# A class of its own for experts with at most 64 rows, in two 64-column groups of TensorE

## The chip, the cores and the metric

The kernel runs on one core of a Trainium2 chip. The metric is the device time of one execution in microseconds; the time before is the median of three runs. The profile is one further execution, taken by the hardware profiler.

## The reference, cut to what matters

A two-layer transformer step over 384 tokens (128 context, 256 latent; width 1024) in fp32. Layer 0 ends in a dense SwiGLU, layer 1 in a top-2-of-8 expert SwiGLU, and the change touches only the latter:

```python
logits = (t @ w_router).astype(jnp.float32)
top_v, top_i = lax.top_k(logits, TOP_K)          # TOP_K = 2, 8 experts
...
for e in range(N_EXPERTS):
    out = out + combine[:, e:e + 1] * swiglu(t, w_gu[e], w_d[e])
def swiglu(x, w_gu, w_d):
    g, u = jnp.split(x @ w_gu, 2, axis=-1)       # 1024 -> 2 x 2816
    return (jax.nn.silu(g) * u) @ w_d            # 2816 -> 1024
```

Only the rows that chose an expert need its product. With the reference's inputs the eight experts get 98, 55, 106, 107, 71, 38, 158 and 135 rows (768 = 2 x 384). Each expert's weights are 34.6 MB, read once.

## The kernel before, in words

**The stream.** All weights come as chunks of 128 x 2048 fp32 (1 MB, two DMAs of 512 KB, issued by SP at L542) through a ring `raw` of RING = 6 buffers. SP issues chunk n once TensorE has finished chunk n-6 (`s_pe`). An expert has 33 chunks: 22 of gate and up (blocks of 512 columns, four chunks a block; the last block of 256 has two chunks with narrower pieces) and 11 of down.

Each product is three matmuls (`three`, L1576 to L1578): hi by hi, hi by lo, lo by hi, of 128 x 128 by 512 columns; a chunk is 12 of them for one tile of 128 rows.

**Experts and classes.** Routing on DVE counts the rows per expert and writes a class number into `ntile`. SHAPES lists the classes: (1, 0) up to 128 rows, (1, 1) up to 160, (2, 0) up to 256, (3, 0) up to 384. In (1, 1) the rows past 128 (at most 32) go another way: `xsum` and `hsum`, unsplit fp32, are multiplied with the `raw` chunk itself in four groups of 32 columns of the array (L2105, L2138), which write four quarters of the PSUM partitions; only chunks 0 and 1, which are split before the class is known, are taken as `whi` and `wlo`. `by_tiles` writes, on each of PE, ACT and DVE, the code of every class one after the other, and within a class that of the eight experts; after an expert, `leave` reads the next expert's class and branches to that class's code for it. The next expert of the same class follows directly.

**Order within an expert.** PE goes through 22 gate/up chunks; after the fifth of each next block it transposes the finished gated block (`turn`, L2072), and ACT and DVE bring it to `hhi` and `hlo`. Then 11 down chunks, between which the next expert's gathered rows are transposed (`gathered`, L2051). ACT and DVE split two chunks of the next expert before they leave one. At the end ACT copies the result to `f` (L933), GpSimd scatters it to `y_rows` (L734) and gathers the rows of the expert after next to `hx` (L709). `s_glo`, `s_ye`, `s_yst`, `s_more` and `s_mored` order the next expert's start.

Of the kernel before, what the change touches and what calls it, by code (L numbers as in the profile page):

```python
# [37 lines left out]
ROWS = 4  # L38
SCALE = HD ** -0.5
QUARTER = P // 4  # L40
SHAPES = [(1, 0), (1, 1), (2, 0), (3, 0)]

# [72 lines left out]
def build(nc, x_prompt, x_sample, cache_k, cache_v, c, c_ctx, w_ada, b_ada, norm_g, w_in, w_out, rpb,  # L115
          g_v, w_s, b_s, w_conv, w_ffn_gu, w_ffn_d, w_router, w_moe_gu, w_moe_d,
          y_prompt, y_sample, new_k, new_v, h_rows, y_rows, rpb_rows):
    with ExitStack() as ctx:
# [323 lines left out]
        def units(b):  # L442

            return min(2 * b + 2, GU_B)
# [30 lines left out]
        def gated_part(T, t, b):  # L475

            return gated[:, 0:block_width(b)] if T == 1 else f[:, t, 0:block_width(b)]

        def rest_width(b):
# [270 lines left out]
        def _(act):  # L750
# [125 lines left out]
            def gathered(e, i):  # L876

                act.wait_ge(s_ga, KT * e + 4 * i + 4)
                act.activation(xhi[:, 4 * i:4 * i + 4, 0:P], gathered_banks(i), ACT.Copy).then_inc(s_ghi, 4)

            def expert(T, quarter, e):

                n0, k = PLACE["exp", e, 0], e + 1

                def silu(b):
# [178 lines left out]
        def _(dve):  # L1064
# [181 lines left out]
            def near_sum(t):  # L1246
# [4 lines left out]
                dve.scalar_tensor_tensor(out=hx[:, t, :], in0=y_near[1][:, t, :], scalar=near_gates[:, 1, t:t + 1],  # L1251
                                         in1=hx[:, t, :], op0=ALU.mult, op1=ALU.add).then_inc(s_near_d, 1)

            def expert(T, quarter, e):

                n0, k = PLACE["exp", e, 0], e + 1
                over = e if quarter else None

# [248 lines left out]
            for t in range(NT):  # L1507
# [62 lines left out]
        def _(pe):  # L1570
# [474 lines left out]
            def gathered(e, i):  # L2045

                if i == 0:
                    pe.wait_ge(s_hx, 16 * NT * e)
                for k in range(4):
                    kt = 4 * i + k  # L2050
                    ins = pe.transpose(ps[:, 6 + i, P * k:P * k + P], hx[:, 0, P * kt:P * kt + P], ident[:, :])  # L2051
                ins.then_inc(s_ga, 4)

            def expert(T, quarter, e):

                n0, k = PLACE["exp", e, 0], e + 1

                def turn(b):
# [220 lines left out]
```

## Time and profile before

| | |
|---|---|
| median of 3 runs | 1615.28 us (1614.29 to 1617.17) |
| the profiled execution | 1618.33 us, span of its trace 1616.6 us |
| TensorE busy | 1557.5 us, 96% of the span |
| VectorE, ScalarE busy | 1031.7 us (64%), 872.7 us (54%) |
| expert stage | from 759.5 us to the end |
| moved by DMA | 425.02 MB, mean 263 GB/s |

Times of rows are in us from the start of the span. PE is TensorE's matmul side, PEld its weight load, DVE VectorE, ACT ScalarE, SP the engine that issues the chunk loads. One fp32 matmul shows as two records. A matmul's duration includes its run through the array, so the distance of starts tells the rate. "issue" is idle time for which the profile shows no releaser.

### The profile page before, as it was taken

How to read it: one execution, taken by the hardware profiler on the slowest of the kernel's cores; microseconds unless marked ns; L12 is line 12 of the kernel's file. 1: busy time of each engine (PE TensorE's matmuls, PEld its weight loads, DVE VectorE, ACT ScalarE, POOL GpSimd, SP SyncE). 2: the span in 40 equal slices, each digit the busy share in tenths (PEclk: the TensorE clock that was granted, in tenths of full speed). 3: DMA queues.
4: the chain of work that ended last, by engine and by line, in shares of the span. 5: the costliest groups of instructions: out<-in, count | busy, mean ns of one | idle time of the engine just before them, and what ended most of it. 6: DMA issues, size and time to landing. Idle time of an engine off the chain costs nothing.

```text
span 1616.6 us, 24317 instructions
## 1 busy us (share of the span) xinstructions
PE 1557.5 (96%) x10076; PEld 1229.6 (76%) x10076; DVE 1031.7 (64%) x935; ACT 872.7 (54%) x886; POOL 164.9 (10%) x180
## 2 busy tenths in 40 slices
PE   6999999999999999998999999999999999999994
PEld 3677777777777778777888888888888878778872
DVE  1445574333422464557888889888888966666665
ACT  2435453222322454545777777777777755555553
POOL 2400000000000220012102030110303010001001
PEclk9999999999999999999999999999999999999998
DMA  9973325666665473233999999999999987878871
GB/s 330 335 264 143 94 84 170 222 210 211 229 241 201 126 246 112 85 125 129 381 371 382 383 367 387 372 379 376 379 383 372 388 323 254 272 265 302 271 283 69
DMA packets 214762, 425.02 MB, mean 263 GB/s; under 512 B 21986, under 2 KB 62946, under 8 KB 214528
## 3 DMA queue, kind: packets, MB, share of 16 engines
q1 hardware_dynamic: 200448, 397.99, 69.4%
q0 software_dynamic: 13056, 22.71, 4.7%
q10 hardware_dynamic: 1136, 2.64, 0.4%
q8 instruction: 84, 1.38, 0.4%
q14 instruction: 38, 0.31, 0.1%
HBM read 418.56 MB, written 22.41 MB: 273 GB/s over the span
## 4 chain that ended last, share of the span: by engine, by line
PE 90%; DVE 4%; DMA 2%; SPq 2%; ACT 1%; issue 1%; POOL 0%; DVEq 0%; ACTq 0%; POOLq 0%
PE ps L1576 26%; PE ps L1578 25%; PE ps L1577 25%; PE ps L2105 3%; PE ps L1620 2%; DMA raw<-in_w_in_dram 1%; SPq L542 1%; PE ps L2138 1%; PE ps L2072 1%; DVE wlo L1072 1%; PE ps L1736 1%; ACT whi L760 1%; PE ps L1767 1%; PE ps L1751 1%; DVE f L1166 1%
## 5 line engine op out<-in xcount | busy, mean ns | idle before, releaser
L1072 DVE TENSOR_TENSOR wlo<-raw,whi 128x2048 fp32r<-128x2048 f32 x327 | 745.4, 2289 | 319.2 <-ACT whi L760 228.1
L760 ACT ACTIVATE whi<-raw 128x2048 fp32r<-128x2048 f32 x327 | 626.6, 1918 | 448.2 <-PE ps L1578 222.1
L1576 PE MATMUL ps<-whi,xhi 128*128 128x512 f32 (+1 forms) x1352 | 538.1, 398 | 5.0 <-DVE xlo L1150 2.3
L1578 PE MATMUL ps<-whi,xlo 128*128 128x512 f32 (+1 forms) x1352 | 524.2, 388 | 0.0
L1577 PE MATMUL ps<-wlo,xhi 128*128 128x512 f32 (+1 forms) x1352 | 524.0, 388 | 0.0
L1576 PEld LDWEIGHTS ps<-whi,xhi 128*128 128x128 f32 x1352 | 255.2, 189 | 68.8 <-issue 15.1
L1578 PEld LDWEIGHTS ps<-whi,xlo 128*128 128x128 f32 x1352 | 255.1, 189 | 53.2
L1577 PEld LDWEIGHTS ps<-wlo,xhi 128*128 128x128 f32 x1352 | 255.5, 189 | 47.8 <-issue 0.5
L1576 PE MATMUL ps<-whi,hhi 128*128 128x512 f32 x484 | 193.9, 401 | 2.6 <-DVE wlo L1072 2.6
L1578 PE MATMUL ps<-whi,hlo 128*128 128x512 f32 x484 | 189.4, 391 | 0.0
L1577 PE MATMUL ps<-wlo,hhi 128*128 128x512 f32 x484 | 189.4, 391 | 0.0
L1576 PEld LDWEIGHTS ps<-whi,hhi 128*128 128x128 f32 x484 | 91.2, 189 | 24.1 <-issue 3.5
L1578 PEld LDWEIGHTS ps<-whi,hlo 128*128 128x128 f32 x484 | 91.3, 189 | 19.7
L1577 PEld LDWEIGHTS ps<-wlo,hhi 128*128 128x128 f32 x484 | 91.4, 189 | 18.1 <-issue 0.2
L734 POOL DMA_INDIRECT y_rows<-f,lidx x24 | 35.4, 1476 | 655.9 <-ACT f L933 400.4
L1620 PE MATMUL ps<-raw,cS 128*32 128x512 f32 x384 | 52.2, 659 | 15.5 <-DMA raw<-in_w_ada_dram 15.5
L709 POOL DMA_INDIRECT hx<-h_rows,lidx x21 | 44.3, 2111 | 9.4 <-issue 6.1
L1620 PEld LDWEIGHTS ps<-raw,cS 128*32 128x32 f32 x384 | 10.2, 114 | 43.2 <-issue 23.3
L905 ACT ACTIVATE hhi<-ps 128x512 fp32r<-128x512 f32 (+1 forms) x48 | 26.3, 548 | 26.9 <-PE ps L2072 13.6
L992 ACT ACTIVATE pr<-ps 128x512 f32<-128x512 f32 (+1 forms) x36 | 19.8, 557 | 37.6 <-PE ps L1578 37.5
L1110 DVE TENSOR_TENSOR f<-ps,f 128x512 f32<-128x512 f32 x12 | 8.3, 690 | 49.1 <-PE ps L1620 49.1
L2105 PE MATMUL ps<-raw,xsum 128*32 128x128 f32 x1280 | 39.0, 274 | 0.0
(245 smaller groups left out, 1090.2 us busy)
## 6 DMA issues: line engine op xcount, KB each, us to landing
raw<-in_w_moe_gu_dram SPq DMA_DIRECT2D x352, 512.0 KB, 5.6
raw<-in_w_moe_d_dram SPq DMA_DIRECT2D x176, 512.0 KB, 5.1
raw<-in_w_ada_dram SPq DMA_DIRECT2D x96, 512.0 KB, 5.1
raw<-in_w_in_dram SPq DMA_DIRECT2D x44, 512.0 KB, 5.3
raw<-in_w_ffn_gu_dram SPq DMA_DIRECT2D x44, 512.0 KB, 6.8
raw<-in_w_ffn_d_dram SPq DMA_DIRECT2D x22, 512.0 KB, 7.0
raw<-in_w_out_dram SPq DMA_DIRECT2D x16, 512.0 KB, 4.2
bias<-rpb_rows POOLq DMA_DIRECT2D x32, 96.0 KB, 4.9
```

Source lines behind the costliest of these rows:

```text
L542: sp.dma_start(to, of).then_inc(s_raw[n % RING], 16)
L709: pool.indirect_dma_start(out=hx[:, i, :], out_offset=None, in_=h_rows[:, :], in_offset=bass.IndirectOffsetOnAxis(ap=lidx[:, e, i:i + 1], ...
L734: pool.indirect_dma_start(out=y_rows[:, :], out_offset=bass.IndirectOffsetOnAxis(ap=lidx[:, e, i:i + 1], axis=0), in_=f[:, i, :], in_offse ...
L760: act.activation(whi[m % SPL][:, :], raw[n % RING][:, :], ACT.Copy).then_inc(s_hi, 1)
L905: act.activation(hhi[:, kts.start:kts.stop, 0:P * T], ps[:, bank, 0:P * T * len(kts)].rearrange("p (k n) -> p k n", k=len(kts)), ACT.Copy) ...
L992: act.activation(pr[:, t, 512 * b:512 * b + width], ps[:, t, 0:width], ACT.Copy).then_inc(s_pr, 1)
L1072: dve.tensor_tensor(wlo[n % RING][:, :], raw[n % RING][:, :], whi[NTH[n] % SPL][:, :].bitcast(F32), ALU.subtract).then_inc(s_lo, 1)
L1576: pe.matmul(out, a_hi, w_hi, start=start, stop=False)
L1577: pe.matmul(out, a_hi, w_lo, start=False, stop=False)
L1578: return pe.matmul(out, a_lo, w_hi, start=False, stop=stop)
L1620: ins = pe.matmul(ps[32 * k:32 * k + 32, bank, :], cS[:, 4 * h + k, :], w[:, k, :], start=(h == 0), stop=(h == 1))
L2105: ins = pe.matmul(o, xsum[:, kt, P:P + QUARTER], m, start=(kt == 0 and i == 0), stop=(kt == KT - 1 and i == len(weights) - 1))
```

## The change

A fifth class (0, 0), for at most HALF = 64 rows, is put first in SHAPES. Such an expert's chunks from the third on are not split: PE multiplies `raw` with `xsum` and `hsum` in two groups of 64 columns of the array, the two halves of a block's columns side by side in the two halves of the PSUM partitions. ACT keeps silu and the final copies, DVE the products and plain copies. The semaphores that splits would have raised are raised in one step. At its end each engine splits the next expert's two first chunks as before. The routing gets one more comparison. The diff, cut to its core:

```diff
-SHAPES = [(1, 0), (1, 1), (2, 0), (3, 0)]
+HALF = P // 2
+SHAPES = [(0, 0), (1, 0), (1, 1), (2, 0), (3, 0)]
...
@@ scalar
+            def half_expert(e):
+                n0, k = PLACE["exp", e, 0], e + 1
+                act.sem_inc(s_morea, KT)
+                act.sem_inc(s_hhi, FK)
+                for b in range(LAST_BLOCK + 1):
+                    act.wait_ge(s_pe, n0 + gate_done(b) + 1)
+                    act.wait_ge(s_ht, FK * k + 4 * (b - 1) if b > 1 else FK * k)
+                    act.activation(half_gated(b), half_gate(b), ACT.Silu
+                                   ).then_inc(s_sg, units(b) - units(b - 1) if b else 2)
+                act.sem_inc(s_hi, N_FFN - 2)
+                state["n"] = n0 + N_FFN
...
+                upto(n0 + N_FFN + 1)
...
+                act.wait_ge(s_pe, n0 + N_FFN)
+                for j in range(2):
+                    ins = act.activation(f[0:HALF, 0, 512 * j:512 * j + 512],
+                                         ps[HALF * j:HALF * j + HALF, DOWN_BANK, :], ACT.Copy)
+                ins.then_inc(s_ye, 1)
...
@@ vector
+            def half_expert(e):
+                n0, k = PLACE["exp", e, 0], e + 1
+                dve.wait_ge(s_glo, KT * (e + 1))
+                for i in range(2):
+                    ins = dve.tensor_copy(xsum[:, 4 * i:4 * i + 4, 0:HALF], gathered_banks(i)[:, :, 0:HALF])
+                ins.then_inc(s_mored, KT)
...
+                for b in range(LAST_BLOCK + 1):
+                    mult(b)
+                    copy(b)
+                dve.sem_inc(s_lo, N_FFN - 2)
+                state["n"] = n0 + N_FFN
...
+                upto(n0 + N_FFN + 1)
...
-            chain(dve.tensor_scalar(cnt[:, :], ps[:, 3, 0:NE], float(P), None, ALU.is_gt))
+            chain(dve.tensor_scalar(cnt[:, :], ps[:, 3, 0:NE], float(HALF), None, ALU.is_gt))
+            chain(dve.scalar_tensor_tensor(out=cnt[:, :], in0=ps[:, 3, 0:NE], scalar=float(P), in1=cnt[:, :],
+                                           op0=ALU.is_gt, op1=ALU.add))
...
@@ tensor
+            def half_expert(e):
...
+                def weights(c, k):
+                    n = n0 + c
+                    if c < 2:
+                        pe.wait_ge(s_lo, NTH[n] + 1)
+                        return [v.bitcast(F32) for v in halves(n, k)]
+                    pe.wait_ge(s_raw[n % RING], 32 * (n // RING + 1))
+                    return [raw[n % RING][:, :].rearrange("p (k n) -> p k n", k=k)]
+                def gate_up_chunk(c):
+                    b, part = divmod(c, 4)
+                    if c == 0:
+                        pe.wait_ge(s_mored, KT * (e + 1))
...
+                    for kk in range(4):
+                        kt = 4 * (part % 2) + kk
+                        for i, v in enumerate(ws):
+                            for j in range(2):
...
+                                ins = pe.matmul(o, xsum[:, kt, 0:HALF], m, start=(kt == 0 and i == 0),
+                                                stop=(kt == KT - 1 and i == len(ws) - 1))
+                    pe_done(ins)
...
+                        for j in range(2):
+                            ins = pe.matmul(ps[HALF * j:HALF * j + HALF, DOWN_BANK, :], hsum[:, kt, 0:HALF],
+                                            w[:, i, 512 * j:512 * j + 512], start=(kt == 0), stop=(kt == FK - 1))
...
             def expert(T, quarter, e):
+                if T == 0:
+                    return half_expert(e)
```

## Rows read from the trace of the kernel before

**Rows 1.** The page's part 1: busy time, share of the span, instructions of each engine
```profile
PE 1557.5 (96%) x10076; PEld 1229.6 (76%) x10076; DVE 1031.7 (64%) x935; ACT 872.7 (54%) x886; POOL 164.9 (10%) x180
```

**Rows 2.** Windows, experts 1, 5 and 6: length, busy per engine, clock, DMA share, GB/s
```profile
853.30:946.80 93.50, 93.28 (x426) 76.82 (x425) 82.27 (x48) 70.50 (x48) 10.47 (x6) 1.00 1.03 378
...
1227.60:1321.20 93.60, 93.60 (x428) 77.11 (x427) 82.75 (x48) 70.43 (x48) 12.93 (x6) 1.00 1.03 379
1321.70:1459.00 137.30, 134.17 (x1388) 104.72 (x1387) 84.97 (x61) 71.52 (x54) 6.02 (x6) 0.98 0.77 261
```

**Rows 3.** Timelines of PE, ACT and DVE from expert 5 to 6: start, length, operation, idle before
```profile
1318.16 0.39 PE L1576 MATMUL ps<-whi,hhi 128*128 128x512 f32 x1
1318.84 0.39 PE L1576 MATMUL ps<-whi,hhi 128*128 128x512 f32 x1
...
1324.85 1.06 PE L2032 MATMUL ps<-ident,hx 32*128 32x32 f32 x8 [3.13 <-issue]
...
1327.29 0.63 PE L1576 MATMUL ps<-whi,xhi 128*128 128x512 f32 x1
...
1328.57 0.63 PE L1576 MATMUL ps<-whi,xhi 128*128 128x512 f32 x1
...
1321.76 1.02 ACT L933 ACTIVATE f<-ps 128x1024 f32<-128x1024 f32 x1 [0.74 <-PE ps L1578]
1327.53 1.91 ACT L760 ACTIVATE whi<-raw 128x2048 fp32r<-128x2048 f32 x1 [4.75 <-issue]
...
1321.05 2.29 DVE L1072 TENSOR_TENSOR wlo<-raw,whi 128x2048 fp32r<-128x2048 f32 x1 [0.42 <-ACT whi L760]
1326.02 0.42 DVE L1210 COPY xsum<-ps 128x256 f32<-128x256 f32 x1 [2.68 <-PE ps L2032]
```

**Rows 4.** Windows with the DMA full: the head, and three parts of expert 1
```profile
34.00:44.00 10.00, 8.98 (x63) 5.96 (x61) 3.32 (x6) 2.54 (x3) 0.00 (x0) 0.83 1.05 387
875.00:895.00 20.00, 20.00 (x94) 16.56 (x93) 18.46 (x12) 15.15 (x11) 0.00 (x0) 1.00 1.05 387
906.00:912.00 6.00, 6.00 (x28) 4.94 (x28) 5.27 (x5) 4.89 (x5) 0.00 (x0) 1.00 1.02 404
898.00:904.00 6.00, 6.00 (x29) 4.95 (x27) 5.38 (x4) 4.08 (x3) 0.00 (x0) 1.00 1.06 354
```

**Rows 5.** Windows of 1 us from expert 5 to 6: the last three columns are clock, DMA, GB/s
```profile
1324.00:1325.00 1.00, 0.15 (x2) 0.15 (x2) 0.00 (x0) 0.00 (x0) 0.69 (x2) 0.64 1.03 383
...
1327.00:1328.00 1.00, 1.00 (x4) 0.81 (x3) 0.00 (x0) 0.47 (x1) 0.69 (x2) 0.50 0.48 150
...
1331.00:1332.00 1.00, 1.00 (x29) 0.78 (x32) 0.00 (x0) 0.00 (x0) 0.14 (x1) 0.94 0.23 34
...
1336.00:1337.00 1.00, 1.00 (x28) 0.75 (x19) 1.00 (x1) 0.97 (x1) 0.00 (x0) 1.00 0.98 121
```

**Rows 6.** Timeline of PE in expert 6: fp32 matmuls in four groups of 32 columns
```profile
1331.22 0.43 PE L2105 MATMUL ps<-whi,xsum 128*32 128x128 f32 x8
...
1334.74 1.93 PE L2105 MATMUL ps<-raw,xsum 128*32 128x128 f32 x64
```

**Rows 7.** SP's waits, expert 1 and then expert 5 to 6: total, times, longest
```profile
SPq L542 <- PE ps L1578: 64.6, 33, 2.4
...
SPq L542 <- PE ps L2105: 12.3, 1, 12.3
```

**Rows 8.** Timeline of PE in the head: one chunk of w_ada, four groups of 32 columns
```profile
18.97 1.94 PE L1620 MATMUL ps<-raw,cS 128*32 128x512 f32 x8 [1.29 <-DMA raw<-in_w_ada_dram]
...
29.70 1.07 PE L1620 MATMUL ps<-raw,cS 128*32 128x512 f32 x8 [2.37 <-DMA raw<-in_w_ada_dram]
```

**Rows 9.** Timelines of DVE, ACT and PE at the start of expert 0
```profile
750.98 0.17 DVE L1533 SCALAR_TENSOR_TENSOR cnt<-ps,cnt 128x8 f32<-128x8 f32 x1
...
759.38 1.92 ACT L760 ACTIVATE whi<-raw 128x2048 fp32r<-128x2048 f32 x1 [0.74 <-issue]
...
759.50 0.50 PE L1576 MATMUL ps<-whi,xhi 128*128 128x512 f32 x1 [1.54 <-DVE xlo L1203]
```

More of the change, by code:

```diff
@@ L477, in gated_part, with half_gated, half_gate, half_up @@
             return gated[:, 0:block_width(b)] if T == 1 else f[:, t, 0:block_width(b)]
+        DOWN_BANK = 4
+        def half_gated(b):
+            return gated[:, 256 * (b % 2):256 * (b % 2) + block_width(b) // 2]
+        def half_gate(b):
+            return ps[:, 2 * (b % 2), 0:block_width(b) // 2]
+        def half_up(b):
+            w = block_width(b) // 2
+            return ps[:, 2 * (b % 2) + 1, 0:w] if b < LAST_BLOCK else ps[:, 2 * (b % 2), w:2 * w]
         def rest_width(b):
@@ L879, in gathered @@
                 act.activation(xhi[:, 4 * i:4 * i + 4, 0:P], gathered_banks(i), ACT.Copy).then_inc(s_ghi, 4)
+            def half_expert(e):
[9 more added lines that the diff above has]
+                state["n"] = n0 + N_FFN
+                for q in range(FK // 2):
+                    if e < NE - 1 and q in GATHER_AT:
+                        gathered(e + 1, GATHER_AT[q])
+                    if e == NE - 1 and 7 <= q < 7 + NT:
+                        near_sum(q - 7)
+                upto(n0 + N_FFN + 1)
+                if e == 0:
+                    act.wait_ge(s_scat, 16 * 2 * NT)
+                else:
+                    act.wait_ge(s_yst, 16 * NT * e)
+                act.sem_inc(s_ye, NT - 1)
+                act.wait_ge(s_pe, n0 + N_FFN)
[3 more added lines that the diff above has]
+                ins.then_inc(s_ye, 1)
             def expert(T, quarter, e):
+                if T == 0:
+                    return half_expert(e)
                 n0, k = PLACE["exp", e, 0], e + 1
@@ L1252, in near_sum, with mult, copy @@
                                          in1=hx[:, t, :], op0=ALU.mult, op1=ALU.add).then_inc(s_near_d, 1)
+            def half_expert(e):
[4 more added lines that the diff above has]
+                ins.then_inc(s_mored, KT)
+                def mult(b):
+                    dve.wait_ge(s_sg, GU_B * k + units(b))
+                    dve.wait_ge(s_pe, n0 + up_done(b) + 1)
+                    dve.tensor_tensor(half_gated(b), half_gated(b), half_up(b), ALU.mult
+                                      ).then_inc(s_pm, units(b) - units(b - 1) if b else 2)
+                def copy(b):
+                    n = ktiles(b) // 2
+                    dve.wait_ge(s_hhi, FK * (k + 1))
+                    dve.wait_ge(s_ht, FK * k + 4 * b + ktiles(b))
+                    for i in range(n):
+                        ins = dve.tensor_copy(hsum[:, 4 * b:4 * b + 2 * n, 0:HALF].rearrange("p (j i) n -> p i j n", i=n)[:, i],
+                                              ps[:, 6 + b % 2, P * i:P * i + P].rearrange("p (j n) -> p j n", j=2))
+                    ins.then_inc(s_hlo, ktiles(b))
+                for b in range(LAST_BLOCK + 1):
[3 more added lines that the diff above has]
+                state["n"] = n0 + N_FFN
+                for q in range(FK // 2):
+                    if e < NE - 1 and q in GATHER_AT:
+                        gathered(e + 1, GATHER_AT[q])
+                    if e == NE - 1 and 7 <= q < 7 + NT:
+                        near_sum(q - 7)
+                upto(n0 + N_FFN + 1)
             def expert(T, quarter, e):
+                if T == 0:
+                    return half_expert(e)
                 n0, k = PLACE["exp", e, 0], e + 1
@@ L2054, in expert @@
             def expert(T, quarter, e):
+                if T == 0:
+                    return half_expert(e)
                 n0, k = PLACE["exp", e, 0], e + 1
```

43 lines of the change are left out of this document (added).

## The prediction

> **What bounds the kernel now.** First the page's part 1 [rows 1]: TensorE is busy 96% of the span. Then the table by expert [rows 2]: there it is busy all the time at full granted clock, but the DMA's share is 1.03 as well, so busy shares alone can't say what a faster expert is worth. The durations can. The copy of an expert's result (L933) cuts the stage: each of experts 1 to 5 takes 93.6 us (expert 0 about as much), whatever its row count (98, 55, 106, 107, 71, 38), with PE busy all of it: TensorE is the bound. Expert 6 (158 rows; 7 has 135) takes 137 us. The counts are the reference's routing on its own inputs. The 93.6 us are worked out thus: three matmuls of 512 columns start every 0.68 us [rows 3], 0.227 each, and 33 chunks x 12 are 89.9 us; 22 transposes of the hidden block and 8 of the next rows do the rest. The DMA moves 378 GB/s meanwhile and is held back only by TensorE: in expert 1's time SP waits 33 times for a chunk's last matmul, 64.6 us in all [rows 7]. What it can do alone stands in [rows 4]: 387 GB/s both in the head, where nothing holds it, and in the gate/up part of an expert; 404 in the down part, whose rows are longer; 354 at the last, narrow gate/up block. A chunk is 1.049 MB, so 2.71, 2.60 and 2.96 us against TensorE's 2.73 us plus transposes. The cover of TensorE is thin: the DMA is the next bound, 3 to 4 us per expert behind.
>
> **The change part by part.** Only experts 1 and 5 have at most 64 rows: two experts of eight change class. Let t0 be the end of the expert before (PE's last matmul).
>
> *Matmuls.* Removed: 12 x 33 matmuls, per expert, and all but two splits on ACT (1.92) and DVE (2.29). Added: per gate/up chunk 4 steps of two groups at once, 64 columns of the array each, 256 columns streamed in fp32; chunks 0 and 1 have 8 steps (whi and wlo); a down chunk has 2 steps of 512. The nearest row is the over class: four groups of 128 columns; 16 such steps (chunks 0 and 1, whi and wlo) fill 1331.22 to 1334.74, 0.22 us each [rows 6]. By columns 0.43 us a step, 1.72 a chunk, 3.44 for chunks 0 and 1: 60 us per expert instead of 90. Loads then bound it. Bound below: no gain in overlap, 0.86 a step (a rival).
>
> *Change of class: the cost that the diff doesn't show.* Each class has its own code for all eight experts; from 5 to 6 the engines leave one for another [rows 3]. PE stands still 3.13 us ("issue"); ACT's next split starts 5.8 us after its last copy began (4.75 idle, "issue"), DVE is ready at most 5.0 us after its last split began. Between experts of one class nothing of it is seen, as the 93.6 show. The Trainium skill, "Runtime: NRT & Kernel Launch", section on instruction fetch mechanics, says that a taken branch to code outside the engine's fetched blocks stops it for a fetch; the trace agrees as to 5 to 6, and the page's rule speaks against this change. There is one such jump on the path before; afterwards five: to expert 0 (the new class's code now stands first), 0 to 1, 1 to 2, 4 to 5, and the old 5 to 6.
>
> *Start of expert 0.* PE now begins 1.54 us after its last pick matmul, set by DVE [rows 9]. With the jump it begins up to 1.6 later, and its clock may fall as it did in the 3.1 us stop [rows 5]: up to 2.4 more for 12 matmuls. ACT's first split there (759.38) starts 0.74 us after its last copy, which had begun at 758.05; 5.8 after that is 763.8, and with 1.92 and 2.29 chunk 2 has its wlo at 768.0 against 765.0 needed. I take +2.7, between 0.5 and 5. The routing's extra DVE operation stands in the chain that pick waits for: +0.2, as its twin L1533.
>
> *Entry of a half expert.* DVE: last split begins t0-0.7, jump to t0+4.3, two xsum copies of 0.42 [rows 3]: PE begins chunk 0 at t0+5.1. At 5 to 6 the clock fell to 1.2 GHz 2.7 us after PE stopped and rose at 1331.1, t0+9.4 [rows 5]. The same here: from 5.1 to 9.4 steps of 0.86, five; three more of 0.43: chunk 0 ends at t0+10.6 (8.5 if the clock stays up, 12.0 if it stays low; 6.5 if DVE is quick too). Only then may SP load chunk 6 into the ring of six. What was issued by t0 lasts to t0+5.7: at 5 to 6 the DMA's share fell to 0.48 in 1327 to 1328, so it ran dry about 1327.4; SP waited 12.3 us for L2105 [rows 7]; the release came at 1334.7 [rows 6], and in 1336 to 1337 the DMA had just begun again, at 121 GB/s [rows 5], 1.6 us later. So loads resume at t0+12.2; about 6 us of DMA time are lost, some 2 of it used by the scatter and gather of rows (98 and 106 of 4 KB, 0.84 MB). Chunk 6 lands at 14.9, chunk 7 (released at 14.0) at 18.3. From there the DMA doesn't stop: 12 chunks of 2.71, 2 of 2.96, 11 of 2.60, and the next expert's chunk 0: 69.7. It lands at X = t0+88.0. PE's idle time before each chunk (about 1 us of 2.7) is covered by that; so is a low clock of some chunks, since the ring holds six.
>
> *Exit to expert 2.* The next chunk must be split after it lands, with nothing ahead: ACT 1.92, DVE 2.29: PE begins at X+4.2 = 92.2, its jump lying under that wait. It has stood 5 us, so 12 matmuls at 0.427 (the spacing at 5 to 6 [rows 3]): 97.3, chunk 1 to 100.3. ACT splits chunk 1 at X+2.7, copies f, jumps: next split at 96.5 (5.8 after dispatch) to 98.6 (4.75 after the copies' end), so wlo of chunk 2 is ready at 100.7 to 102.8. I take 101.5; before, chunk 2 began at 93.6+5.5 = 99.1. That is **+2.4 us**, although the half expert itself is shorter.
>
> *Exit to expert 6.* There the jump was paid already: PE's transposes for the class ended at 1325.9, 4.1 after t0, so chunk 0 began at 93.6+4.1 = 97.7 [rows 3]; now at 92.2; its four column groups keep PE from chunk 2 until 10.8 us later, 103.0, when ACT and DVE are ready. **-5.5 us.** What follows to the end is bound by TensorE and keeps it.
>
> **Sum:** +2.7 +0.2 +2.4 -5.5 = -0.2 us. The profiled execution took 1618.33 us with a span of 1616.6, 3.05 above the median of 1615.28; the sum is a difference and goes on the median: 1615, say 1615.5. Two terms hang on X, so each us in X counts twice.
>
> **The rivals.**
> - *Clearly faster (1607).* The entry is cheap: code arrives in time, PE starts at t0+3.1 with its clock up, chunk 0 ends at 6.5, X = 84: -1.6 at expert 2, -9.5 at expert 6, +2.9 at the start. For it: DVE's 5.0 is only an upper bound. Against: the clock fell within 3.1 us at 5 to 6. With no entry loss at all X would be 82, the total 1603. Chance of over 0.2% faster: 0.29.
> - *Slower (1621).* The low clock of the entry lasts for all of chunk 0 (12.0, X = 89.4, +2.8 in two places), and chunk 2 of expert 2, waiting for ACT behind its jump, lets the clock fall once more (+2.4), or the start costs its 5. It decides from X = 89.7 on. Chance of over 0.2% slower, with the next two: 0.29.
> - *The clock stays at 1.2 GHz in the half experts (1685).* A step of 0.86 makes 3.44 a chunk, above the load's 2.71, and 35 such are 120 us: some +35 per half expert. For it: in the head a chunk of four fp32 matmuls took 1.93 us, then 1.07 later on [rows 8]; before the short one PE had worked without a pause, before the long ones it had waited for loads. Against: at 3.44 PE never waits, and after unbroken work it rose each time. 0.03. The Trainium skill, "TensorE: Matmul & The Clock Gate", section on HAM oscillation, describes this for thin matmuls that wait for loads; no row here shows it in a warm stretch.
> - *Two groups don't run at once (1685),* the same price. Four do [rows 6]. 0.02.
> - *The DMA holds no more than the 354 GB/s of its lowest row* [rows 4] *over a whole half expert.* A chunk is 2.96, 25 chunks or so are 7 us more per half expert: 1629. Against: 20 us in a row at 387. 0.02, in the slower part. The Trainium skill, "DMA: Bandwidth & Descriptors", Specifications, names about 358 GB/s as HBM's limit for a core; the trace shows more than that.
>
> **How the numbers follow.** 0.2% (3.2 us) is what a measurement here can tell. No change has 0.42, faster 0.29, slower 0.29. The range runs from the cheap entry to a little past the long one: 1607 to 1623, about 0.8.
>
> **What the profile after would show.** Experts 2, 3, 4 again at 93.6; two experts with splits only at their ends and DMA at 385 or more over most of them; PE idle of 3 us or more at each change of class, 5 us at each half expert's start; SP waiting about 11 us for chunk 0 there; low clock after each; chunk 0 of expert 2 about 92 after t0. Wrong would be: PE steps of 0.86 at full clock; no gap at a change of class; a DMA rate in the half experts above 400 or below 375, which moves X by 2 to 3 us.

## The result and the profile after

The kernel after takes 1626.72 us, median of 4 runs (1624.47 to 1628.29), against 1614.85 us for the kernel before in 4 runs beside it: ratio 1.007, 95% interval 1.0052 to 1.0087. The forecast of 1615.5 us, no change, was wrong, and the time lies above its range. The profiled execution took 1626.89 us with a span of 1625.1, which is 8.5 above the span of before.

The page's part 1 of the kernel after, for [rows 1]:

```profile
PE 1515.2 (93%) x10206; PEld 1149.5 (71%) x10206; DVE 890.1 (55%) x888; ACT 748.4 (46%) x814; POOL 152.6 (9%) x180
```

Every engine that computes has less to do (TensorE 42 us, DVE 142, ACT 124) and the kernel is longer. So the loss lies in idle time, and a table by stage finds it. A stage ends where ACT starts to copy an expert's result to `f` (L980; L922 in the half class, L933 before); expert 0 counts from the end of the last pick matmul. In us:

| expert | 0 | 1 | 2 | 3 | 4 | 5 | 6 | 7 |
|---|---|---|---|---|---|---|---|---|
| before | 95.54 | 93.92 | 93.58 | 93.58 | 93.58 | 93.60 | 137.37 | 130.80 |
| after | 99.70 | 96.05 | 96.45 | 93.64 | 93.62 | 94.46 | 136.95 | 130.80 |
| difference | +4.16 | +2.13 | +2.87 | +0.06 | +0.04 | +0.86 | -0.42 | 0.00 |

They sum to +9.7; the part ahead of the experts was 1.1 shorter in this execution, as single executions differ (its length is 754.1 to 760.7 us over the traces of this case). The medians are 11.9 apart, so some 2 us of the loss stand in no stage of these two traces. One thing to know in reading the table: ACT copies a half expert's result only behind both splits of the next expert, 5.2 us after PE's last matmul, so this wait counts to the half expert's own stage.

Windows of the kernel after, experts 1, 2, 5 and 6 (columns as in [rows 2]):

```profile
856.54:952.59 96.05, 72.82 (x491) 37.49 (x491) 11.04 (x23) 8.14 (x12) 6.02 (x6) 0.94 0.99 365
952.59:1049.04 96.45, 96.21 (x427) 79.36 (x428) 83.65 (x48) 70.84 (x51) 10.15 (x6) 0.97 1.02 372
1236.30:1330.76 94.46, 70.74 (x491) 36.01 (x491) 11.04 (x23) 8.13 (x11) 6.01 (x6) 0.98 1.00 368
1330.76:1467.71 136.95, 134.65 (x1389) 104.95 (x1389) 85.76 (x61) 71.77 (x56) 6.32 (x6) 0.98 0.77 267
```

A half expert keeps PE busy 71 to 73 us and still lasts 94 to 96: its DMA share is 1, its rate 365 to 368 GB/s against 378 in [rows 2]. The expert behind it has PE busy all through and takes 2.9 us more than a plain one: work at a low clock, mean 0.97.

**The start of expert 0.** Timelines of PE, ACT and DVE, for [rows 9]:

```profile
754.78 2.06 PE L2104 MATMUL ps<-pick,f 128*128 128x128 f32 x17
760.74 0.77 PE L1664 MATMUL ps<-whi,xhi 128*128 128x512 f32 x1 [3.90 <-issue]
761.30 0.63 PE L1665 MATMUL ps<-wlo,xhi 128*128 128x512 f32 x1
...
762.12 1.91 ACT L776 ACTIVATE whi<-raw 128x2048 fp32r<-128x2048 f32 x1 [4.59 <-issue]
...
765.85 2.29 DVE L1119 TENSOR_TENSOR wlo<-raw,whi 128x2048 fp32r<-128x2048 f32 x1 [6.18 <-issue]
```

Three engines stand still with nothing in the timelines to wait for, 3.9, 4.6 and 6.2 us. PE had 1.54 in [rows 9]. Then it starts at low clock: matmuls 0.43 us apart until 763.4.

**Entry of half expert 1.** Timelines of PE and DVE, then windows of 2 us:

```profile
861.13 1.12 PE L2188 MATMUL ps<-whi,xsum 128*64 128x256 f32 x4 [4.63 <-DVE xsum L1306]
862.04 1.07 PE L2188 MATMUL ps<-wlo,xsum 128*64 128x256 f32 x4
...
866.16 0.60 PE L2188 MATMUL ps<-whi,xsum 128*64 128x256 f32 x4
...
860.33 0.76 DVE L1306 COPY xsum<-ps 128x256 f32<-128x256 f32 x2 [2.20 <-issue]
```
```profile
866.00:868.00 2.00, 2.00 (x22) 1.32 (x20) 0.00 (x0) 0.00 (x0) 0.00 (x0) 1.00 0.04 0
868.00:870.00 2.00, 2.00 (x22) 1.29 (x20) 0.00 (x0) 0.00 (x0) 0.00 (x0) 1.00 0.76 219
870.00:872.00 2.00, 2.00 (x22) 1.28 (x20) 0.00 (x0) 0.39 (x1) 0.00 (x0) 1.00 0.91 319
872.00:874.00 2.00, 2.00 (x22) 1.32 (x20) 0.00 (x0) 0.00 (x0) 0.00 (x0) 1.00 0.89 306
874.00:876.00 2.00, 2.00 (x22) 1.32 (x20) 0.42 (x1) 0.00 (x0) 0.00 (x0) 1.00 0.97 333
876.00:878.00 2.00, 2.00 (x20) 1.07 (x18) 0.00 (x0) 0.35 (x1) 0.00 (x0) 1.00 1.02 376
```

t0 is 861.13 - 4.63 = 856.50. PE begins at t0+4.6, a row of four records (two fp32 matmuls, one to each half of the array) costs 0.86 us at low clock and 0.43 at full, chunk 0 is done at 867.02, t0+10.5: all as forecast. At 866 to 868 the DMA is dry, and behind it the rate climbs slowly: it is at 376 GB/s only 9 us after chunk 0's release.

**How late the next chunk is.** The DMA's queue q1 (all chunk loads) from chunk 0's release (867.02) to the landing of the next expert's chunk 0 (948.08):

```profile
q1 hardware_dynamic: 14069, 30.60, 101.4%
```

That takes 81.06 us where the forecast had 77.4. The 28 chunks that had to move are 29.36 MB; 30.60 were moved. So 1.24 MB of later chunks had already arrived when the awaited one was complete, worth 3.2 us at 385 GB/s.

**Exit to expert 2.** Timelines of ACT and PE:

```profile
948.08 1.91 ACT L776 ACTIVATE whi<-raw 128x2048 fp32r<-128x2048 f32 x1 [9.63 <-DMA raw<-in_w_moe_gu_dram]
950.77 1.91 ACT L776 ACTIVATE whi<-raw 128x2048 fp32r<-128x2048 f32 x1 [0.78 <-DMA raw<-in_w_moe_gu_dram]
952.59 1.18 ACT L922 ACTIVATE f<-ps 64x512 f32<-64x512 f32 x2
953.67 1.90 ACT L776 ACTIVATE whi<-raw 128x2048 fp32r<-128x2048 f32 x1
...
952.83 0.77 PE L1664 MATMUL ps<-whi,xhi 128*128 128x512 f32 x1 [5.41 <-DVE wlo L1119]
...
958.09 0.43 PE L1664 MATMUL ps<-whi,xhi 128*128 128x512 f32 x1
```

PE waits 5.4 us for the landing and two splits, then twelve matmuls run 0.43 apart. ACT shows no jump.

**Exit to expert 6.** Timeline of PE, for [rows 3] and [rows 6]:

```profile
1330.91 1.05 PE L2120 MATMUL ps<-ident,hx 32*128 32x32 f32 x8 [5.32 <-issue]
1331.90 0.80 PE L1664 MATMUL ps<-whi,xhi 128*128 128x512 f32 x1
...
1337.83 0.43 PE L2268 MATMUL ps<-whi,xsum 128*32 128x128 f32 x8 [0.54 <-DVE xsum L1257]
...
1341.34 0.61 PE L2268 MATMUL ps<-raw,xsum 128*32 128x128 f32 x12
1343.56 1.69 PE L2268 MATMUL ps<-raw,xsum 128*32 128x128 f32 x51 [1.60 <-issue]
```

The jump stands in full, 5.32 us where it was 3.13 [rows 3], and a second stop of 1.60 follows.

**What ends these stops.** The timelines name no releaser, but the trace holds DMA packets of the kind "instruction". View of the DMA queues in the kernel after, 1328.31 to 1329.42, inside the stop of 5.32 us:

```profile
q8 instruction: 1, 0.02, 6.2%
```

It is one packet of 16 KB, and such a packet lies ahead of the end of each stop of PE:

| run | PE stands still | packet of q8 | from its end to PE's next start |
|---|---|---|---|
| before | 1321.72 to 1324.85 | 1322.36 to 1323.37 | 1.48 |
| after | 756.84 to 760.74 | 757.77 to 759.03 | 1.70 |
| after | 1325.59 to 1330.91 | 1328.32 to 1329.42 | 1.49 |
| after | 1341.95 to 1343.56 | 1341.15 to 1342.07 | 1.48 |
| e1_never | 1326.90 to 1328.34 | 1325.91 to 1326.96 | 1.38 |

The traces of this case have 13 stops of PE on "issue" of 1.4 to 5.4 us at or just behind a change of class, and in all of them PE goes on 1.4 to 1.7 us after the end of a packet of q8, though such packets come 3 to 44 us apart. (Two of 1.54 us at the start of expert 0, in e2_order and e13_limit48, aren't counted: other traces put the same 1.54 down to DVE.) ACT and DVE go on 1.4 to 1.8 us after the end of an 8 KB packet of q14. So these stops are waits for code, as far as an order of events can show it, and their lengths differ by when the load of the code begins: from 1.0 before PE stops to 2.8 after. The run e1_never is described below.

### The profile page after: what moved, and what is told of

The parts are those of the page before. It is cut to its first block, busy times and chain, and to the rows that moved or that the text cites. A ratio compares the mean times of both kernels' runs of the same rounds, so it can differ in the third digit from the quotient of the medians.

```text
span 1625.1 us, 24366 instructions
## 1 busy us (share of the span) xinstructions
PE 1515.2 (93%) x10206; PEld 1149.5 (71%) x10206; DVE 890.1 (55%) x888; ACT 748.4 (46%) x814; POOL 152.6 (9%) x180
## 4 chain that ended last, share of the span: by engine, by line
PE 80%; DMA 9%; DVE 4%; issue 2%; ACT 2%; SPq 2%; DVEq 0%; POOL 0%; ACTq 0%; POOLq 0%
PE ps L1664 22%; PE ps L1666 21%; PE ps L1665 21%; DMA raw<-in_w_moe_gu_dram 4%; PE ps L2268 3%; PE ps L2188 3%; PE ps L1708 2%; DMA raw<-in_w_moe_d_dram 2%; SPq L558 2%; DMA raw<-in_w_in_dram 1%; PE ps L2301 1%; ACT whi L776 1%; DVE wlo L1119 1%; PE ps L2235 1%; PE ps L1824 1%
## 5 line engine op out<-in xcount | busy, mean ns | idle before, releaser
L1119 DVE TENSOR_TENSOR wlo<-raw,whi 128x2048 fp32r<-128x2048 f32 x265 | 604.0, 2290 | 323.8 <-ACT whi L776 229.7
L776 ACT ACTIVATE whi<-raw 128x2048 fp32r<-128x2048 f32 x265 | 507.8, 1918 | 437.8 <-PE ps L1666 206.8
L1664 PE MATMUL ps<-whi,xhi 128*128 128x512 f32 (+1 forms) x1176 | 470.1, 400 | 13.5 <-DVE wlo L1119 7.3
L1666 PE MATMUL ps<-whi,xlo 128*128 128x512 f32 (+1 forms) x1176 | 456.8, 388 | 0.0
L1665 PE MATMUL ps<-wlo,xhi 128*128 128x512 f32 (+1 forms) x1176 | 456.5, 388 | 0.0
L1664 PE MATMUL ps<-whi,hhi 128*128 128x512 f32 x396 | 159.0, 401 | 2.6 <-DVE wlo L1119 2.6
L1666 PE MATMUL ps<-whi,hlo 128*128 128x512 f32 x396 | 155.0, 391 | 0.0
L2188 PE MATMUL ps<-raw,xsum 128*64 128x256 f32 x640 | 76.6, 389 | 17.4 <-DMA raw<-in_w_moe_gu_dram 17.4
L2188 PEld LDWEIGHTS ps<-raw,xsum 128*64 128x64 f32 x640 | 46.1, 139 | 45.6 <-DMA raw<-in_w_moe_gu_dram 16.7
L2204 PE MATMUL ps<-raw,hsum 128*64 128x512 f32 x176 | 42.6, 601 | 10.3 <-DMA raw<-in_w_moe_d_dram 10.2
```

What stands on the lines that cost most here:

```text
L776: act.activation(whi[m % SPL][:, :], raw[n % RING][:, :], ACT.Copy).then_inc(s_hi, 1)
L1119: dve.tensor_tensor(wlo[n % RING][:, :], raw[n % RING][:, :], whi[NTH[n] % SPL][:, :].bitcast(F32), ALU.subtract).then_inc(s_lo, 1)
L1664: pe.matmul(out, a_hi, w_hi, start=start, stop=False)
L1665: pe.matmul(out, a_hi, w_lo, start=False, stop=False)
L1666: return pe.matmul(out, a_lo, w_hi, start=False, stop=stop)
L2188: ins = pe.matmul(o, xsum[:, kt, 0:HALF], m, start=(kt == 0 and i == 0), stop=(kt == KT - 1 and i == len(ws) - 1))
```

## The experiments

Where a run was timed against the kernel before on its chip, its ratio is given with the interval. The runs fell on several chips. On some, expert 7 takes 130.8 us, on others 135.2 to 138, whatever the kernel (and the kernel before takes 1614.6 to 1614.9 or 1622.5 to 1623.4 us in all); so stages of experts 6 and 7 are compared within a chip only, those of experts 0 to 5 anywhere. Each chip was used in one session, so what is called a chip here may as well be the session.

### Do the jumps cost, and do the stages add up?

```diff
 e1_never:  no expert is ever of the half class
-ps[:, 3, 0:NE], float(HALF), None, ALU.is_gt
+ps[:, 3, 0:NE], 0.0, None, ALU.is_gt
 e2_order:  the 128 class's code stands first
-            leave(1, 0)
-            for kind, shape in zip(kinds, SHAPES):
+            leave(2, 0)
+            for kind in (2, 1, 3, 4, 5):
+                shape = SHAPES[kind - 1]
 e13_limit48:  e2_order, and only expert 5 (38 rows) is a half expert
-ps[:, 3, 0:NE], float(HALF), None, ALU.is_gt
+ps[:, 3, 0:NE], 48.0, None, ALU.is_gt
 e14_after:  the kernel after, unchanged
```

> The changed kernel, with the first comparison of the counts at 0 instead of 64 rows: no expert takes the new class, but its code still stands first. If the loss at the start is the jump over that code (my theory, 4.1 us between the last pick matmul and the end of expert 0 in the changed kernel), this kernel is about 4 us slower than the one before (1619), with PE idle near 3.9 us before expert 0's first matmul and 93.6 us for each of experts 1 to 5. If the code's place costs nothing and the whole loss sits in the half experts, it is equal to the one before (1615).

> The changed kernel with the code of the 128-row class placed first and that of the 64-row class second, nothing else. Theory: only the jump to expert 0 goes, so it is 4 us faster than the changed kernel (1622 to 1623) and the jumps 0 to 1, 1 to 2, 4 to 5 and 5 to 6 stay as they are. Rival (the place of code doesn't matter): 1626.7.

> The kernel after with two edits: the limit of the half class is 48 rows instead of 64 (so expert 1 with 55 rows keeps the 128 class and only expert 5 with 38 changes), and the 128 class's code comes first. If the loss of 11.9 us is the sum of its stages, this takes away the start (4.2), the entry of expert 1 and its thin gain turned loss (2.1) and the exit to expert 2 (2.9); left are expert 5 (+0.9) and expert 6 (-0.4): ratio 1.0003, same as before. Rival: classes changed in the middle cost as much wherever they are, and only the start comes back: 1.0035.

> The kernel after, unchanged, beside the two straight versions on one chip, because expert 7 took 130.8 us on some chips and 136 on others whatever the kernel. Stages as in its first profile if the chip is one of the first kind: start 99.7, expert 1 96.0, expert 2 96.5, expert 5 94.5, expert 6 136.9; ratio 1.007. On a chip of the other kind expert 7 takes 136 here and in the kernel before, and the ratio is again 1.006 to 1.007.

| | ratio | experts 0, 1, 2, 5, 6 |
|---|---|---|
| e1_never | 1.0026 (1.0015 to 1.0036) | 100.62, 93.95, 93.66, 93.59, 136.87 |
| e2_order | 1.0019 (1.0007 to 1.0031) | 95.56, 96.22, 96.82, 92.89, 137.16 |
| e13_limit48 | 0.9988 (0.998 to 0.9997) | 95.52, 93.92, 93.59, 93.91, 137.28 |
| e14_after | 1.0047 (1.0033 to 1.0062) | 99.71, 95.71, 95.44, 93.82, 137.27 |

With no half expert at all, the place of the code alone costs 0.26%, and expert 0 has its jump (PE idle 3.92 us on "issue"). Its jump from expert 5 to 6 stops PE for 1.44 us where the kernel before has 3.13. With the other class's code first, expert 0 takes 95.56 as before. In that run the entry of expert 5, a change of class like the others, costs nothing: PE begins 2.34 us after t0, as without branches (4.4 in the kernel after). The limit of 48 also brings expert 1 and 2 back to 93.92 and 93.59. Experts 0 to 2 of e14_after are 7.8 us above those of e13_limit48, and the kernels 9.0 apart (1631.21 and 1622.20). So the loss lies in its stages, most of it in those of experts 0 to 2, and the change at expert 5 costs about nothing. That e13_limit48 comes out 0.12% faster than before has no counterpart in the stages and is within what can be told here.

### What is the half class worth without branches?

The branches were replaced by straight code for these inputs' classes, with the half class and with the 128 class in its place.

```diff
 e3_straight_half (also e15_straight_half, e18_straight_half); the whole of the branching code goes
+            for e, shape in enumerate([(1, 0), (0, 0), (1, 0), (1, 0), (1, 0), (0, 0), (1, 1), (1, 1)]):
+                part(*shape, e)
 e4_straight_128 (also e16_straight_128, e17_straight_128)
+            for e, shape in enumerate([(1, 0)] * 6 + [(1, 1)] * 2):
+                part(*shape, e)
```

> The changed kernel without classes at run time: the code of the eight experts stands in one line, each in the class that these inputs give it (128, 64, 128, 128, 128, 64, over, over), no class is read and no branch is taken. Theory: all the jumps go. PE begins a half expert about 2.5 us after the end of the one before (4.6 and 4.4 in the changed kernel), its clock up or down for less of chunk 0, chunk 6 is loaded 3 to 5 us earlier, expert 6 begins without its stop of 5.3 us; but the 5 us stop before expert 2 (land, split on ACT, split on DVE) stays, and its low clock. Sum: 12 to 16 us faster than the changed kernel, 1611 to 1615. Rival (loads are what holds the half experts, jumps lie under them): at most 5 us faster, 1621 or more.

> The kernel before in one line in the same way: experts 0 to 5 in the 128-row class, 6 and 7 in the over class, no branch. It is the base for the straight half kernel. The only jump of the one before (5 to 6: 3.1 us of PE and a low clock, some 5 us in all) goes: 1610. If the straight half kernel is no faster than this one, the half class gains nothing even without jumps.

> The half class in straight code, as run before on another chip (0.9998 there). If this chip's expert 7 takes 130.8, theory A (TensorE is starved of instructions in the over class's small matmuls only on some chips) expects expert 6 at 130.8 to 131.5 without any added matmuls, and ratio 0.9965. Theory B (the added matmuls took the gaps away) expects 136.8 and 1.000. If expert 7 takes 136 here, both expect 1.000.

> The 128 class alone in straight code (0.9996 on another chip). On a chip whose expert 7 takes 130.8: theory A expects expert 6 at 130.8 as well, ratio 0.996, the same as the straight half class: then all of that gain is the one branch of the kernel before and none the half class's. Theory B expects 137 and 1.000. The difference of the straight versions is what the half class brings when no branch disturbs it: by the stages seen, 0 to -1 us.

> The 128 class alone in straight code, once more, for the case that this chip is of the kind whose expert 7 takes 130.8 us. Theory A (the instruction supply falls short only on the other kind of chip) then expects expert 6 at 130.8 and ratio 0.996; theory B (only added matmuls take the gaps away) 137 and 1.000. With expert 7 at 136 both expect 1.000.

> The straight version with both half experts, on the same chip. With expert 7 at 130.8: A expects expert 6 at 130.8 to 131.5, ratio 0.9963 to 0.997, within 1.5 us of the straight 128 version; B expects 136.8 and 1.000. With expert 7 at 136 both expect 0.9995.

| | ratio | experts 1, 2, 5, 6, 7 |
|---|---|---|
| half, three chips | 0.9998 (0.9988 to 1.0009) | 93.31, 96.42, 92.65, 136.78, 136.09 |
| | 0.9993 (0.998 to 1.0005) | 91.96, 95.47, 92.82, 138.45, 136.42 |
| | 0.9992 (0.9981 to 1.0002) | 93.13, 96.23, 92.73, 136.85, 137.98 |
| 128, the same chips | 0.9996 (0.9986 to 1.0006) | 93.57, 93.58, 93.60, 137.99, 135.62 |
| | 0.9999 (0.999 to 1.0008) | 93.60, 93.60, 93.63, 137.81, 135.82 |
| | 1.0002 (0.9991 to 1.0013) | 93.56, 93.57, 93.57, 138.24, 135.67 |

With no branch anywhere the half class still gives nothing that can be measured: its own two stages gain 0.3 to 1.6 and 0.8 to 1.0 us, and expert 2 gives back 1.9 to 2.8. PE starts 2.3 us after t0 there, its clock falls for a moment, and chunk 0 is done at t0+7.5 to 7.7 (in one of the six half experts the clock stays up, and it is t0+6.0): about the fast entry that the forecast's first rival had. It doesn't pay, because of what stands at the other end: the next expert's chunk 0 lands at t0+87.5 to 88.8 (88.3 in the one with 6.0), where that rival had 84.

The 128 version shows a second thing: taking away the one branch of the kernel before gives nothing either on these chips. Timeline of PE in e4_straight_128, expert 6:

```profile
1325.29 0.40 PE L2081 MATMUL ps<-wlo,xsum 128*32 128x128 f32 x8
1325.98 0.44 PE L2081 MATMUL ps<-whi,xsum 128*32 128x128 f32 x4 [0.29 <-issue]
1326.73 0.33 PE L2081 MATMUL ps<-whi,xsum 128*32 128x128 f32 x2 [0.31 <-issue]
...
1328.16 0.45 PE L2081 MATMUL ps<-wlo,xsum 128*32 128x128 f32 x5 [0.99 <-issue]
1328.92 0.27 PE L2081 MATMUL ps<-wlo,xsum 128*32 128x128 f32 x1 [0.31 <-issue]
1329.62 0.29 PE L2081 MATMUL ps<-wlo,xsum 128*32 128x128 f32 x1 [0.44 <-issue]
```

These 16 steps took 3.5 us in a row in [rows 6]. Here they dribble at a few records per 0.7 us, waiting for nothing in the profile. The same lines stop in expert 7, but the stops that the profile shows there (1.9 to 2.8 us) are only part of what the 135.2 to 138 us have over 130.8. On the chip of the first traces there were no such short stops. Unlike the stops at a change of class they don't end at a fixed distance behind a packet of q8, and their cause stays open.

### Is it the depth of the loads?

```diff
 e5_straight_3loads (e12_straight_2loads: n - 2), on the straight half version, in SP's loop
+                m = n - 3
+                if STREAM[n][0] == "exp" and STREAM[m][0] == "exp":
+                    sp.wait_ge(s_raw[m % RING], 32 * (m // RING + 1))
```

> The straight half kernel with one wait more on SP: within the experts a chunk is issued only when the chunk three before it has landed, so at most three are in flight instead of five or six. In the changed kernel and in the straight one the next expert's chunk 0 lands 81 us after the first chunk of a half expert is released (80.5, 81.1, 81.3), where I had reckoned 77.4 from a queue that delivers chunk after chunk. Theory: with five chunks in flight the DMA engines work on several at once, and a chunk lands some 3 us after its bytes' turn; with three in flight it lands earlier: 78 to 79.5 us, so the two half experts are 1.5 to 3 us shorter each. Rival (the extra is lost DMA time at the start of the expert, the depth of the queue means nothing): 81 us or more, since a shallower queue can only cost.

> Straight code with both half experts, but at most two chunks of an expert under load at once. Theory: the awaited chunk lands late because the chunks behind it move bytes at the same time (1.24 and 0.8 MB ahead by the count of bytes); with two under load at most one can be ahead: release of chunk 0 to landing of the next chunk 0 falls from 80.5 to 81.3 to about 79, if the rate stays at 385 or more. Rival: the rate falls with two under load (each has a start-up), and the time is 82 or more, the kernel slower than the straight version (1622).

Chunk 0's release to the next chunk 0's landing took 80.5 us in both half experts with three chunks under load, as with the full ring (79.95 to 82.5 in the straight half versions), though the median time from issue to landing was 6.8 us (10.5 in the kernel after). With two it took 86.8 and 86.9, at 354 GB/s where three had 382, and the kernel 1659.08 us (one execution), since every expert slows down: experts 2 to 5 take 98.9 to 100.7. Queue q1 between the two points, with three and then two under load:

```profile
q1 hardware_dynamic: 13906, 30.28, 101.0%
```
```profile
q1 hardware_dynamic: 13879, 30.21, 97.1%
```

29.36 MB were needed each time, so 0.9 MB ran ahead in both, a little under a chunk. My first idea, a deep queue in which the awaited chunk shares with all behind it, is wrong; so is its repair, that fewer loads bring it sooner. One chunk beside the awaited one is always under way, and fewer cost rate. e5_straight_3loads took 1609.05 us in one execution against 1614.57, with expert 6 at 133.38.

### Can the low clock at the exits be bought off?

```diff
 e6_straight_warm: 20 small fp32 matmuls at the end of each half expert (straight half version)
+                warm(20, 5)
 e11_half_warm_last: the same, before expert 6 only
 e10_half5_warm: the same, only expert 5 a half expert
 e9_128_warm: in e4_straight_128, before expert 6 only
+                if e == 5:
+                    warm(20, 3)
```

> The straight half kernel with 20 transposes' worth of matmuls on the identity (4.6 us of work, result unused) at the end of each half expert, in the 5.0 us in which PE waits for the next expert's first split. Theory: the clock stays at 2.4 GHz, so expert 2 takes 93.6 us instead of 96.4, and the expert after the second half expert 1 to 3 us less: 4 to 5 us faster than the straight half kernel, which had the same time as the one before: ratio 0.997. Rival (the 2.8 us of expert 2 come from the thin lead of the loads, not from the clock): no change.

> No branches and no half class (as the straight version with the 128 class only, whose expert 6 took 137.99 us), but 20 small fp32 matmuls of TensorE (4.7 us) on a free bank between expert 5 and expert 6. Theory A: the 137 us of expert 6 hold a stretch of some 6 us in which TensorE stands still on 'issue' in the over class's small column-group matmuls, because instructions come in slower than it uses them; long enough easy work ahead of it gives the supply a lead. Then the gaps are gone, expert 6 takes 130.8 plus the 4.7 of the added work, that is 135.5 against 138, and the kernel gains 2 us (ratio 0.9985) without any half expert. Rival B: what took the gaps away was the half expert before it (fewer instructions, loads standing still), not the added matmuls: then the gaps stay, expert 6 takes 142 and the kernel loses 4.5 us (1.003).

> No branches; only expert 5 is a half expert, expert 1 keeps the 128 class; the 20 small matmuls at the end of expert 5. If the gain of the straight version with added matmuls (0.9963) comes at the exit to expert 6 and the half expert 1 brings about nothing (-1.3 in itself, +2.1 in expert 2), this gives expert 1, 2 at 93.6, expert 5 about 92.6, expert 6 130.8: 1 us less and 6.6 less, ratio 0.9955 to 0.996. If instead expert 1's half class brings its share, the ratio is 0.998 or more.

> As the straight version with both half experts and added matmuls, but these only before expert 6, none before expert 2. If the added matmuls matter only for the over class's instruction supply, expert 2 takes 96.4 (instead of 95.7) and the rest stays: ratio 0.9967. If the clock at expert 2 had been worth the 2.4 us that the prediction gave it, the ratio is 0.9978.

| | ratio | experts 1, 2, 5, 6, 7 |
|---|---|---|
| e6_straight_warm | 0.9963 (0.995 to 0.9975) | 92.20, 95.71, 92.57, 130.81, 130.80 |
| e9_128_warm | 1.0002 (0.9994 to 1.0011) | 93.60, 93.60, 93.60, 137.04, 136.41 |
| e10_half5_warm | 0.9983 (0.9975 to 0.9992) | 93.56, 93.57, 92.15, 138.14, 135.17 |
| e11_half_warm_last | 1.0005 (0.9996 to 1.0014) | 93.05, 96.21, 91.78, 138.96, 136.42 |

Timeline of ACT in e6_straight_warm, expert 2:

```profile
949.27 1.92 ACT L752 ACTIVATE whi<-raw 128x2048 fp32r<-128x2048 f32 x1 [0.61 <-DMA raw<-in_w_moe_gu_dram]
951.98 1.92 ACT L752 ACTIVATE whi<-raw 128x2048 fp32r<-128x2048 f32 x1 [0.79 <-DMA raw<-in_w_moe_gu_dram]
...
955.91 1.92 ACT L752 ACTIVATE whi<-raw 128x2048 fp32r<-128x2048 f32 x1 [1.40 <-DMA raw<-in_w_moe_gu_dram]
```

With the clock kept up, expert 2 takes 95.7 us. Without the added matmuls it takes 96.2 to 96.4 where all of its first twelve matmuls are slow (e3, e11, e18), and 95.5 where some eight are (e15, e5). With the clock up ACT waits for a load 13 times, 12.0 us in all: the half expert hands on a ring with nothing in it, and TensorE at full clock only catches up with the loads. So the clock is worth 0.7 us at most here, not the 2.4 of twelve slow matmuls.

Expert 6 of e6_straight_warm gained 6 us, and I put them down to the added matmuls, which would give the supply of instructions a lead. e10 and e11 have the same matmuls in the same place, and expert 6 takes 138 and 139, its short stops as long as without them (2.8 and 2.9 us; 2.2 to 2.6 in the straight half versions): behind a half expert that theory fell. Behind a 128 expert it didn't quite: in e9 the stops of expert 6 shrink to 0.6 us (3.3 to 3.6 in the 128 versions), and the 137.0, which hold 4.7 us of added work, are neither the 135.5 nor the 142 expected. These three ran on a chip whose expert 7 takes 135.2 to 136.4, e6 on one where it takes 130.8. On e6's chip there is one straight version without them, e5_straight_3loads; PE's waits there, over expert 6:

```profile
PE ps L1643 <- DVE wlo L1098: 4.4, 1, 4.4
```

No stop on "issue" at all, and 133.38: the added matmuls are worth 2.6 us on that chip by one trace of each, about the twelve slow matmuls (2.4), since expert 6 is bound by TensorE and can use the clock. The other 4 us against the kernel before come without them; the wait for the splits (4.4) counts to expert 5 here. Whether the rest is the removed branch alone stays open: the 128 version in straight code never ran on such a chip.

### Half experts side by side

Experts reordered to 1, 5, 0, 2, 3, 4, 6, 7, so that two entries and two exits share one change of class; e8 has e6's added matmuls too.

```diff
+ORDER = [1, 5, 0, 2, 3, 4, 6, 7]
-    return ffn_src(w_moe_gu[0, l], w_moe_d[0, l], j)
+    return ffn_src(w_moe_gu[0, ORDER[l]], w_moe_d[0, ORDER[l]], j)
```

> The changed kernel, classes and branches as they are, with the experts taken in the order 1, 5, 0, 2, 3, 4, 6, 7: the router's columns and the weights are read in that order, the result is the same. The two half experts stand side by side at the start: no jump to the first, none between them, one after them, and the one before the over class. Theory: the second follows at the DMA's pace, 89 us, since five chunks are in flight while its chunk 0 is split; entry and exit are paid once; by stage sums 6 us faster than the kernel before, ratio 0.996. Rival (each half expert costs its own 3 us or more whatever its neighbours): slower than the kernel before by 2 to 8 us.

> The same order with the 20 unused matmuls after each half expert. Theory: after the second half expert PE stands for the split and the jump; the matmuls are queued before the jump and keep the clock up, 2 to 3 us less than the order alone, ratio to the kernel before 0.995. After the first half expert they lie in the wait for the split and change nothing. Rival: the jump holds PE after them anyway and the clock falls then: no gain over the order alone.

e7_together came out at 1.0025 (1.0013 to 1.0038), e8_together_warm at 1.0039 (1.0025 to 1.0053). Both were expected to gain (0.996 and 0.995); the rival held in each. The first three stages of e7_together are 95.13, 93.74 and 97.29, 3.1 us more than before. Timelines of DVE and PE in e7_together, from the first half expert to the second:

```profile
849.90 2.29 DVE L1124 TENSOR_TENSOR wlo<-raw,whi 128x2048 fp32r<-128x2048 f32 x1 [10.78 <-ACT whi L781]
852.61 2.29 DVE L1124 TENSOR_TENSOR wlo<-raw,whi 128x2048 fp32r<-128x2048 f32 x1 [0.42 <-ACT whi L781]
854.82 0.75 DVE L1311 COPY xsum<-ps 128x256 f32<-128x256 f32 x2
...
855.63 1.12 PE L2193 MATMUL ps<-whi,xsum 128*64 128x256 f32 x4 [8.33 <-DVE xsum L1311]
```

No change of class here, yet PE stands 8.3 us: it needs `xsum`, which DVE copies only behind both of the next expert's splits, and the second of these needs the second chunk. Chunk 0 is done only at t0+14.0 there, and the next one lands at t0+94.4. Two half experts in a row have the worst entry of all (a copy of `xsum` ahead of the splits was not tried), and the added matmuls ahead of a jump (e8) only put the jump behind them: expert 0, third there, took 100.2.

## Why the prediction was wrong, step by step

| term | forecast | measured |
|---|---|---|
| start of expert 0 | +2.9 | +4.2 |
| expert 1 and exit to expert 2 | +2.4 | +5.0 |
| expert 5 and exit to expert 6 | -5.5 | +0.4 |
| sum | -0.2 | +9.7, with 0.1 in experts 3 and 4 (medians: +11.9) |

**Right.** The matmul step of 0.43 us and the overlap of two groups; the change of class as the hidden cost, at three of the four new places (from expert 1 to 2 no engine shows it); the entry (t0+10.5 and +9.5 against 10.6); the DMA as the next bound, at 387, about 355 and 404 to 410 GB/s in its parts; experts 3 and 4 untouched. The rivals of a lasting low clock, of groups in turn and of a 354 GB/s DMA are refuted.

**Wrong, first step: "It lands at X = t0+88.0".** It landed at 91.6 and 90.0. The mechanism stood, the size didn't. From release to landing I had 77.4 us. It was 81.06 and 80.44, and 79.4 or more in every version. Two terms were missing. The rate after a dry spell climbs over some 9 us (2.35 MB in the first 9 us after the release, where 385 GB/s give 3.46: 2.9 us lost, against 1.6 assumed). And the bytes that run ahead, 1.24 MB or 3.2 us. With these the sum is 81.9. Each of the two X went into its exit in full.

**Wrong, second step: the exit to expert 6, "now at 92.2 ... -5.5 us".** Of the 5.9 us, X is 2.0. The next 1.4 are the jump. I had it "lying under that wait" of 4.2 us for the splits. It took 5.32 and stood open: PE's chunk 0 began 5.65 after the landing. 0.5 more is DVE, late with `xsum` behind its own jump (4.17 on "issue"), and 1.6 the stop at 1343.56, which the trace of before hasn't. Some 0.4 is left over.

**Mis-sized: the start, +2.7.** The mechanism and place were right, and +4.2 lies inside the 0.5 to 5 given. I took PE's idle time as up to 1.6 more than 1.54, from its 3.13 at 5 to 6; it was 3.90.

**The exit to expert 2** held but for X: from the landing to the first matmul 4.75 (4.2 forecast), twelve at 0.43. The jump of ACT that I added (1.2 us for chunk 2) didn't show.

**The rivals and the chances.** The slower rival named the point, "X = 89.7 on", and both X were beyond it; its own reasons, a clock low for all of chunk 0 and the start at 5 us, weren't what brought X there. It gave 1621, and reached 1623 with the range; the ends of X (82 to 89.4) were drawn around a DMA body that had no range of its own. The bound that was missing is the load's. I had taken the rate of a full DMA from [rows 4] and not asked when the awaited chunk is complete. e3_straight_half and its twins say more: even the cheap entry, worth 1607 by the first rival, gives 0.9992 to 0.9998. The third rival's reading of [rows 8] was loose: its short row (29.70) stands itself behind a wait of 2.37 us.

**A page and a row.** The jumps' length spread from 1.4 to 5.4 us on PE. The Trainium skill, "Runtime: NRT & Kernel Launch", section on instruction fetch mechanics, says that a branch beyond the fetched blocks stalls its engine, and that straight code streams with the fetch mostly hidden. The first half agrees with the rows, at 3.9, 4.6 and 6.2 us on three engines, each ended 1.4 to 1.7 us after a packet of code. The second holds in most straight stretches, where packets of q8 pass without a stop. Straight code did stop in dense small matmuls on the three chips that ran the pairs of straight versions, for 4.6 to 5.9 us in experts 6 and 7 together, but no row ties these short stops to a packet, so whether they speak against it is open.

## What to carry to other kernels

A faster stage between two bounded ones is worth what the next stage can take over: count its entry (what must finish before loads resume), its body by bytes and not by busy time, and its exit, where the stage behind it finds no lead. Here 21 to 23 us less busy time of TensorE per expert became about 1 us (0.3 to 1.6 without branches), and the exit took 2 to 3 back. Put the common path's code first, and allow up to 6 us per engine for each change of code; a jump hides only under a wait longer than itself. An awaited load lands about one load later than the bytes up to it say.

## What the runs showed of the hardware

- A jump to another class's code stopped PE for 1.4 to 5.4 us, ACT for 3.3 to 5.4 and DVE for up to 6.2, the same kind of jump at different lengths in one execution, and once (e2_order, entry of expert 5) not at all. PE went on 1.4 to 1.7 us after the end of a 16 KB packet of kind "instruction", in 13 stops of 13.
- The same code has expert 7 at 130.8 us on some chips and at 135.2 to 138 on others. There PE stops again and again for 0.3 to 1.0 us, some 0.75 us apart, in runs of small fp32 matmuls in four column groups; the stops seen are 1.9 to 2.8 us of the difference.
- Two groups of 64 columns run at once: a step of two fp32 matmuls of 256 columns, one to each group, takes 0.43 us at full clock, 0.86 at half. One alone of 128 columns takes 0.24 us (e6_straight_warm, 20 in 4.73), so two of 256 in turn would take twice the 0.43.
- After a dry spell, with a ring of free buffers, the loads needed 9 us to come back to 376 GB/s.
- Two chunks of 1 MB under load aren't enough for the full rate (354 GB/s), three are (382 over the same stretch, as in straight code with the full ring).
